# The spatial norm's gain and bias moved behind the position mixing, in a two-layer hybrid encoder

## The reference

```python
def spatial_gating(u, v, w_s, b_s, ln_g, ln_b):
    v = layernorm(v, ln_g, ln_b)              # over the 512 features of branch B
    vb = v.reshape(b_, nb, B_BLOCK, B_GROUPS, B_GROUP_DIM)   # 4 blocks of 128 positions, 8 groups of 64 features
    w = jnp.where(mask[None], w_s, jnp.zeros_like(w_s))      # per group 128 x 128 (t, s), chunk-causal
    sv = jnp.einsum('gts,bnsgc->bntgc', w, vb) + b_s.T[None, None, :, :, None]
    return u * sv.reshape(b_, s_, B_WIDTH)
```

## Time and profile before

| | |
|---|---|
| median of 3 runs | 1032.23 us |
| profiled execution | 1032.96 us |
| its span | 1031.1 us |
| TensorE matmuls | 1013.6 us busy, 98% |
| VectorE | 640.6 us, 62% |
| ScalarE | 517.5 us, 50% |
| GpSimd | 287.8 us, 28% |
| mean granted TensorE clock | 0.995 |
| TensorE on the chain that ended last | 93% |

### The profile page before, as it was taken

How to read it: one execution, slowest core, us unless ns; L and a number is a source line. 1 busy time by engine, 2 the same in 40 slices (tenths; PEclk the granted TensorE clock), 3 DMA queues, 4 the chain that set the end, 5 groups by cost and what they waited for, 6 DMA issues and landing times.

```text
span 1031.1 us, 15310 instructions
## 1 busy us (share of the span) xinstructions
PE 1013.6 (98%) x6388; PEld 854.8 (83%) x6388; DVE 640.6 (62%) x840; ACT 517.5 (50%) x804; POOL 287.8 (28%) x144
## 2 busy tenths in 40 slices
PE   7989999999999999999999999999999999999997
PEld 6869899888888888888888989988888888888876
DVE  6888865899543535445628689479983444444552
ACT  6855774766552332223456766577546233332333
POOL 1221113532421413233212111153243232322430
PEclk9989999999999999999999999999999999999999
DMA  6512221222123323224342222212232232323602
GB/s 219 154 63 82 84 68 57 82 82 83 62 63 102 111 90 106 82 82 129 117 133 82 83 83 84 63 61 83 83 102 61 82 103 82 102 84 100 203 2 81
DMA packets 93428, 94.71 MB, mean 92 GB/s; under 512 B 2272, under 2 KB 91568, under 8 KB 93360
## 3 DMA queue, kind: packets, MB, share of 16 engines
q1 hardware_dynamic: 93088, 93.60, 29.3%
q10 hardware_dynamic: 272, 0.14, 0.1%
HBM read 91.64 MB, written 2.10 MB: 91 GB/s over the span
## 4 chain that ended last, share of the span: by engine, by line
PE 93%; DVE 3%; ACT 1%; issue 1%; DMA 1%; ACTq 0%; DVEq 0%
PE pj L504 27%; PE pj L505 26%; PE pj L506 26%; PE mx L641 2%; PE mx L504 1%; PE mx L505 1%; PE mx L506 1%; PE mx L581 1%; PE mx L604 1%; PE mx L701 1%; PE mx L669 1%; PE mx L589 1%; DVE q_rot L1421 1%; PE mx L679 1%; PE mx L672 1%
## 5 line engine op out<-in xcount | busy, mean ns | idle before, releaser
L1161 POOL TENSOR_TENSOR w_lo<-w_raw,w_hi 128x1024 fp32r<-128x1024 f32 (+1 forms) x89 | 196.3, 2206 | 571.6 <-ACT w_hi L818 571.3
L504 PE MATMUL pj<-h_hi,w_hi 128*128 128x512 f32 x832 | 330.2, 397 | 0.0
L506 PE MATMUL pj<-h_hi,w_lo 128*128 128x512 f32 x832 | 324.6, 390 | 0.0
L505 PE MATMUL pj<-h_lo,w_hi 128*128 128x512 f32 x832 | 324.5, 390 | 0.0
L818 ACT ACTIVATE w_hi<-w_raw 128x1024 fp32r<-128x1024 f32 (+1 forms) x179 | 159.1, 938 | 161.3 <-PE pj L506 161.1
L1271 DVE TENSOR_TENSOR w_lo<-w_raw,w_hi 128x1024 fp32r<-128x1024 f32 (+1 forms) x90 | 161.3, 1792 | 70.7 <-ACT w_hi L818 70.4
L504 PEld LDWEIGHTS pj<-h_hi,w_hi 128*128 128x128 f32 x832 | 156.6, 188 | 34.7 <-issue 3.0
L506 PEld LDWEIGHTS pj<-h_hi,w_lo 128*128 128x128 f32 x832 | 156.5, 188 | 33.0
L505 PEld LDWEIGHTS pj<-h_lo,w_hi 128*128 128x128 f32 x832 | 156.7, 188 | 32.1 <-issue 1.0
L1385 DVE TENSOR_TENSOR merge_gate<-pj,rstd 128x512 f32<-128x512 f32 x48 | 33.2, 691 | 162.9 <-PE pj L506 162.9
L936 ACT ACTIVATE merge_gate<-merge_gate,small 128x512 f32<-128x512 f32 x48 | 34.3, 715 | 89.3 <-DVE merge_gate L1385 89.3
(11 more groups left out here) (257 smaller groups left out, 1497.6 us busy)
## 6 DMA issues: line engine op xcount, KB each, us to landing
w_raw<-in_w_in SPq DMA_DIRECT2D x61, 1024.0 KB, 5.5
w_raw<-in_w_branch SPq DMA_DIRECT2D x24, 512.0 KB, 3.4
w_raw<-in_w_out SPq DMA_DIRECT2D x6, 1024.0 KB, 5.2
x_tokens<-in_x SPq DMA_DIRECT2D x4, 512.0 KB, 6.6
w_raw_last<-in_w_out SPq DMA_DIRECT2D x2, 1024.0 KB, 7.7
sp_w_rows<-in_sp_w SPq DMA_DIRECT2D x2, 512.0 KB, 6.4
out<-out_low SPq DMA_DIRECT2D x4, 256.0 KB, 2.0
out<-out_high SPq DMA_DIRECT2D x4, 256.0 KB, 2.3
```

The costliest lines, as they stand in the source:

```text
L504: pe.matmul(bank, wh, ah, start=first, stop=False)
L505: pe.matmul(bank, wh, al, start=False, stop=False)
L506: return pe.matmul(bank, wl, ah, start=False, stop=final)
L1161: return pool.tensor_tensor(out=dst, in0=full, in1=hi.bitcast(f32), op=ALU.subtract)
```

## The change

The norm's g and b are no longer applied to `GV`. They are loaded once for both layers as sixteen more rows of `VR` (two DMAs on ScalarE's queue), transposed with the other vectors and copied to `LNV`, one value per partition for each tile of 128 channels. GpSimd's two operations and SP's broadcast loads go. TensorE makes the row sums of the masked matrices at hook 23, as a product of ones with `WT`, in bank `M[2]`. VectorE, in phase 25, adds b times these sums to `SPB` in place. The evacuation of the mixed result multiplies by g and adds `SPB`.

```diff
-        LNG = at("ln_g", [P, T], r_ob + 4 * KB)
-        LNB = at("ln_b", [P, T], r_ob + 6 * KB)
+        LNV = small[:, 112:128]
-        VR = at("vec_rows", [64, P], r_brl + 12 * KB)
+        VR = at("vec_rows", [80, P], r_brl + 12 * KB)
...
-                sp.dma_start(LNG[:, :], sp_ln_g[layer].partition_broadcast(P)).then_inc(side_in, 16)
-                sp.dma_start(LNB[:, :], sp_ln_b[layer].partition_broadcast(P)).then_inc(side_in, 16)
...
-            pe.wait_ge(vec_in, 16 * 3)
-            pe.transpose(PJ[2][:, 0:64], VR[0:64, :], CST[0:64, 0:64]).then_inc(vecT_done, 1)
+            pe.wait_ge(vec_in, 16 * 5)
+            pe.transpose(PJ[2][:, 0:80], VR[0:80, :], CST[0:80, 0:80]).then_inc(vecT_done, 1)
...
+                def spatial_row_sums():
+                    pe.wait_ge(wT_ready, upto(wT_ready, 1))
+                    pe.wait_ge(oa_evac, upto(oa_evac, 4))
+                    for ct in range(4):
+                        for g in range(2):
+                            last = pe.matmul(M[2][g * HD:(g + 1) * HD, ct * P:(ct + 1) * P], ONE[:, 0:HD],
+                                             WT[:, 2 * ct + g, :], start=True, stop=True)
+                    last.then_inc(rows_summed, 1)
+
                 def spatial(ct):
                     if ct == 0:
-                        pe.wait_ge(wT_ready, upto(wT_ready, 1))
-                        pe.wait_ge(gv_ready, upto(gv_ready, 1))
-                        pe.wait_ge(oa_evac, upto(oa_evac, 4))
+                        pe.wait_ge(ln_scaled, upto(ln_scaled, 1))
+                    if ct == 2:
+                        pe.wait_ge(bias_ready, upto(bias_ready, 1))
...
                 hooks[20].append((transpose_spatial,))
+                hooks[23].append((spatial_row_sums,))
...
+            act.dma_start(VR[64:72, :], sp_ln_g.rearrange("l (k p) -> (l k) p", p=P)).then_inc(vec_in, 16)
+            act.dma_start(VR[72:80, :], sp_ln_b.rearrange("l (k p) -> (l k) p", p=P)).then_inc(vec_in, 16)
...
-                def ln_affine():
-                    pool.wait_ge(side_in, upto(side_in, 16 * 6))
-                    pool.wait_ge(ln_scaled, upto(ln_scaled, 1))
-                    pool.tensor_tensor(out=GV[:, :, :], in0=GV[:, :, :], op=ALU.mult,
-                                       in1=LNG[:, :].unsqueeze(1).to_broadcast([P, TB, T])).then_inc(pool_step, 1)
-                    pool.wait_ge(pool_step, upto(pool_step, 1))
-                    pool.tensor_tensor(out=GV[:, :, :], in0=GV[:, :, :], op=ALU.add,
-                                       in1=LNB[:, :].unsqueeze(1).to_broadcast([P, TB, T])).then_inc(gv_ready, 1)
...
+            dve.tensor_copy(LNV, PJ[2][:, 64:80])
             dve.tensor_copy(LBT[:, 24:32], PJ[2][:, 56:64]).then_inc(p_vec, 1)
...
+                def spatial_bias():
+
+                    dve.wait_ge(side_in, upto(side_in, 16 * 4))
+                    dve.wait_ge(rows_summed, upto(rows_summed, 1))
+                    for ct in range(4):
+                        c = 8 + 4 * layer + ct
+                        last = dve.scalar_tensor_tensor(out=SPB[:, ct, :], in0=M[2][:, ct * P:(ct + 1) * P],
+                                                        scalar=LNV[:, c:c + 1], in1=SPB[:, ct, :],
+                                                        op0=ALU.mult, op1=ALU.add)
+                    last.then_inc(bias_ready, 1)
...
-                        chained(dve.tensor_tensor(out=OX[:, 1, ct, :].rearrange("p (n t) -> p n t", t=P),
-                                                  in0=M[ct % 3][:, :].rearrange("p (n t) -> p n t", t=P),
-                                                  in1=SPB[:, ct, :].unsqueeze(1).to_broadcast([P, TB, P]), op=ALU.add))
+                        g = LNV[:, 4 * layer + ct:4 * layer + ct + 1]
+                        chained(dve.scalar_tensor_tensor(out=OX[:, 1, ct, :].rearrange("p (n t) -> p n t", t=P),
+                                                         in0=M[ct % 3][:, :].rearrange("p (n t) -> p n t", t=P),
+                                                         scalar=g, op0=ALU.mult, op1=ALU.add,
+                                                         in1=SPB[:, ct, :].unsqueeze(1).to_broadcast([P, TB, P])))
...
+                phase[25].append((spatial_bias,))
```

More of the change, by code:

```diff
@@ L232, in build @@
         PER_LAYER = dict(
-            side_in=16 * 6, pj_done=NJ, act_evac=sum(e == "a" for e, _ in EVAC_NO),
+            side_in=16 * 4, pj_done=NJ, act_evac=sum(e == "a" for e, _ in EVAC_NO),
             vec_evac=sum(e == "v" for e, _ in EVAC_NO), norm_sum=1, rstd_ready=1, vT_done=1, va_ready=1, clamped=2,
@@ L239, in build @@
             state_ready=2, oc_done=2, oc_evac=2, ocn_done=2, oc_rstd=2, oc_ready=2, wT_done=1, wT_evac=1, wT_ready=1,
-            ln_stats=1, ln_rstd=1, ln_scaled=1, gv_ready=1, sv_done=4, gated=len(SG_JOBS), br_hi=len(GATE_JOBS),
-            br_lo=len(GATE_JOBS), y_full=KT, y_hi=KT, y_lo=KT, pool_step=1)
+            ln_stats=1, ln_rstd=1, ln_scaled=1, rows_summed=1, bias_ready=1, sv_done=4, gated=len(SG_JOBS), br_hi=len(GATE_JOBS),
+            br_lo=len(GATE_JOBS), y_full=KT, y_hi=KT, y_lo=KT)
         per_layer = {}
@@ L262, in build @@
             lsem(n) for n in ("clamped", "vb_ready", "sg_ready", "gm_ready"))
-        pool_step = lsem("pool_step")
         rope_done, k_swapped = lsem("rope_done"), lsem("k_swapped")
@@ L275, in build @@
         wT_done, wT_evac, wT_ready = lsem("wT_done"), lsem("wT_evac"), lsem("wT_ready")
-        ln_stats, ln_rstd, ln_scaled, gv_ready = lsem("ln_stats"), lsem("ln_rstd"), lsem("ln_scaled"), lsem("gv_ready")
+        ln_stats, ln_rstd, ln_scaled = lsem("ln_stats"), lsem("ln_rstd"), lsem("ln_scaled")
+        rows_summed, bias_ready = lsem("rows_summed"), lsem("bias_ready")
         sv_done = lsem("sv_done")
@@ L683, in transpose_spatial @@
                 def transpose_spatial():
-                    pe.wait_ge(side_in, upto(side_in, 16 * 6))
+                    pe.wait_ge(side_in, upto(side_in, 16 * 4))
                     pe.wait_ge(pT_evac, upto(pT_evac, A_HEADS // 2))
@@ L940, in softmax_exp @@
                     if j == 0:
-                        act.wait_ge(side_in, upto(side_in, 16 * 6))
+                        act.wait_ge(side_in, upto(side_in, 16 * 4))
                     act.wait_ge(negmax_ready, upto(negmax_ready, j + 1))
@@ L1195, in program @@
                 phase = {n: [] for n in range(NJ + 4)}
-                phase[23].append((ln_affine,))
                 for n in GATE_JOBS:
@@ L1661, in sinks @@
                 def sinks():
-                    dve.wait_ge(side_in, upto(side_in, 16 * 6))
+                    dve.wait_ge(side_in, upto(side_in, 16 * 4))
                     chained(dve.tensor_scalar(NSK, SK, -1.0, None, ALU.mult))
```

## The result

The changed kernel took 1035.56 us (median of 7 runs, 1034.66 to 1037.13) against 1032.23 (7 runs, 1031.28 to 1033.52) for the one before: ratio 1.0035, 95% interval 1.0025 to 1.0046. It is slower by 2.6 to 4.7 us. The forecast was 1035.5 in a range of 1033.4 to 1037.3, with 0.72 on slower by more than 0.2%. A second set of 5 runs gave 1036.19, ratio 1.0041 (1.0028 to 1.0054).

What follows compares the result with a forecast made beforehand. TensorE, busy 98% of the span, was taken to bound the kernel. Row sums 2.44 plus start 0.8 plus 0 for the rest gave +3.24 us: 1035.5 on the median of 1032.23, range 1033.4 to 1037.3.

Steps and rivals of the forecast that it cites:

- TensorE as the length; GpSimd's work off the path: Whole kernel: TensorE, 98% busy, sets the length; removing GpSimd's two operations per layer, about 10 us, leaves the sum unchanged.
- Row sums, 2.44: TensorE behind recurrent_out: products of ones take 1.02 us plus 0.20 at the next projection, 1.22 per layer, 2.44 for two.
- fourth rival: TensorE's row sums: products with the same ones run at the dense rate, 0.5 us per layer; total +1.8, 1034.0; chance 0.07.
- VectorE hides its part: VectorE before the level matmuls: bias operations of 1.1 to 1.4 us per layer fit the slack, so nothing waits.
- second rival: VectorE from 230 to 244 us becomes the bound, 0.7 us per layer before the level matmuls; 1036.9; chance 0.12.
- Start, landing, 1.49: Kernel start: two more small loads on ScalarE's queue, 0.74 us each, delay the transpose of the vector rows by 1.49.
- Start, share that reaches the end, 0.8: Of 1.63 us delay at TensorE's first projection, 0.8 reaches the end, the first clock rise staying, the second moving.
- rival 1: TensorE's clock gives the start's delay back, by rises that stay put or a later fall; +2.0, 1034.2; chance 0.24.
- Third rival: Before the query wait: the shift takes apart VectorE's collisions with GpSimd, so not slower; -1.3, 1030.9; chance 0.07.

Runs made afterwards that it cites:

- experiment 1: The kernel before with only the eight products of ones per layer added at hook 23, unread: 1034.10 us, ratio 1.0023.
- experiment 9: The kernel before with four more small vector loads on ScalarE's queue, the transpose of the vector rows waiting for all seven: 1034.13 us, ratio 1.0023.
- Experiment 2: The kernel before with only the change's start: two more vector loads, wait for five, transpose of 80 rows, one more copy: 1033.46 us, ratio 1.0015.
- experiment 6: The changed kernel with the vector-load wait and transpose moved into the first projection, VectorE's four copies moved later: 1034.65 us, ratio 1.0025.
- experiment 8: The changed kernel with the row sums as two products of 512 columns per layer in place of eight of 128: 1035.69 us, ratio 1.0037.

## Why the prediction was right

- **TensorE as the length; GpSimd's work off the path.** Right. The tails show no gain from the removal, to within 0.2 us, and the timelines the collision at VectorE gone (5.07 to 0.68). The GPSIMD Engine Reference of the Trainium skill (Key points) says that GpSimd contends with VectorE instructions that have two SBUF inputs; this trace agrees, and it doesn't matter for the time.
- **Row sums, 2.44.** Right to a hundredth in the chain (1.02 + 0.20 per layer), 2.5 in the tails, +2.4 in the runs of experiment 1. The fourth rival, the dense rate, is refuted.
- **VectorE hides its part.** Right in outcome: no new wait of TensorE. The slack was mis-sized: 0.86 us was counted to the start of the level group, where only its second half needs the last operand (1.9). And the thinner place, `recurrent_out` of the second pair with about 0.5 us to spare, was not in the list: VectorE's 1.1 us are hidden there only because TensorE is 1.2 later too. Past it the second rival's loss would have come, at another place than the rival names. (The rival's own sum, twice 0.7, is 1.4 and not 1.5.)
- **Start, landing, 1.49.** The measured shift of 1.35 us in the first pair of traces looked like a hit. Over the executions it is 0.8 on average, and with four more loads 1.6, where the pace gives 3.0 (experiment 9). Working a pace per load out of two landings of one execution was the weak step. The spread of the landing can't be seen in one profile. The last load of 4 KB took 5.2 to 6.3 us here beside the large ones. The Trainium skill (DMA: Bandwidth & Descriptors, Queues, rings and completion order) says that a semaphore's increment lands only after every earlier write of that DMA engine, across its queues. The long landings fit that, but no run here takes the large loads away, so it is not shown; and the rule doesn't say what one more load costs.
- **Start, share that reaches the end, 0.8.** Experiment 2 has 1.5 to 1.8 (interval 0.7 to 2.5), and experiment 6 gives 1.5 back. The two errors, landing too large and carry too small, worked against each other. That the forecast of 1035.5 meets the 1035.56 of the first set is luck in this part; the second set is 4.5 above the kernel before, and 3.3 and 4.5 both lie in the stated range. The first profiled execution is what rival 1 describes (all of the delay back by 68.4); the timed runs are not.
- **Third rival.** The collisions stayed together, as GpSimd is released by the same chain: the last product of the queries takes 2.73 us in both kernels.

What stays open is why the start costs 1.5 to 1.8 us in the timed runs when the first projection is 0.9 later on average in the traces (11.3 with five loads, 10.4 with three). The tails place the cost ahead of 80 us. The intervals of the experiments, about 0.9 us to each side, would allow both to be 1.

## What to carry to other kernels

In this kernel, 98% TensorE, moving work from an idle engine into a few more matmuls cost just what the matmuls take, and the 20 us freed elsewhere were worth nothing. Look at who stands behind a wait before adding a load to it: 8 KB on the path to the first matmul cost more than half as much as all the row sums, and the same loads with the wait further back cost little or nothing (0.5 us above the row sums, within the interval). And where the same kernel's traces differ in when the clock rises, a difference of under 2 us is to be taken from timed runs, or from a stretch of the traces behind the place where they differ: here the tail repeats to 0.2 us, while the spans of one kernel's runs differ by 2 to 3.

## What was not expected of the hardware

- Weights 64 columns wide, in two halves of the array: 1024 columns of f32 take 1.02 us as eight products or 1.01 as two; with 128-wide weights 1.72. Behind the narrow groups (L692, L707, L638) the next projection matmul takes 0.43 us in the chain in place of 0.23; behind the 128-wide ones (L669 and L676) it does not.
- The last of the vector loads landed at 8.6 to 9.7 us in executions of kernels with the same five loads, with x and the weights on the other queue; in one more (experiment 8) it was there before TensorE asked at 8.16.
- The fall of TensorE's clock in the same idle stretch came at about 62.1 us in one execution and at about 64.7 in another of the same kernel. Behind the same 2.3 us of waiting it fell in one kernel's execution (82 to 84 us, 0.50) and not in another's (1.00).
